# Two-block transformer step on one core: moving the building of the third and fourth block's weight sums to later stages

## The reference, cut to what matters

```python
def second_block(x, c, ...):
    for i in range(2):
        ...
        y = _dsa_mixer(h, ...) if i == 0 else _short_conv_mixer(h, ...)
        x = x + g1 * y
        h = _rmsnorm(x, norm2_g[i]) * (1.0 + sc2) + sh2
        x = x + g2 * ((silu(h @ w_gate[i]) * (h @ w_up[i])) @ w_down[i])
```

## Time and profile before

| | before |
|---|---|
| median of 3 runs | 2673.64 us (2669.71 to 2680.84) |
| the profiled execution's own time | 2684.21 us |
| its span | 2682.4 us |
| PE busy | 2610.3 us (97%) |
| DVE, ACT, POOL busy | 1463.0, 1002.9, 840.7 us |
| mean granted clock of TensorE | 0.986 |
| DMA, software queue | 121.85 MB, 17.4% of the 16 engines' span |
| DMA, hardware queue (SP's loads) | 266.28 MB, 33.2% |

### The profile page before, as it was taken

The page is one execution under the profiler, slowest core; times in us unless marked ns, Lnnn a source line. Parts: engine busy times, 40 slices in busy tenths (PEclk is TensorE's granted clock), DMA queues, the critical chain, the costliest instruction groups (busy, mean ns, idle before and its releaser), DMA issues.

```text
span 2682.4 us, 30812 instructions
## 1 busy us (share of the span) xinstructions
PE 2610.3 (97%) x12482; PEld 2134.7 (80%) x12482; DVE 1463.0 (55%) x2083; ACT 1002.9 (37%) x1606; POOL 840.7 (31%) x702
## 2 busy tenths in 40 slices
PE   9999999999999999999999999969999999999999
PEld 8878887877777778887787666758888888888887
DVE  4343256666666445544577598443336854643366
ACT  4222234334444323422265445522225532322253
POOL 6663025675556678086600241100000000000000
PEclk9999999999999999999999998989999999999999
DMA  6543334455555576364464218899335633333355
GB/s 193 157 142 122 102 115 139 125 159 154 141 134 145 149 204 198 97 177 148 132 210 143 71 48 212 216 265 223 97 94 180 201 92 97 118 103 102 95 167 174
DMA packets 422286, 391.68 MB, mean 146 GB/s; under 512 B 17572, under 2 KB 337312, under 8 KB 422080
## 3 DMA queue, kind: packets, MB, share of 16 engines
q1 hardware_dynamic: 377264, 266.28, 33.2%
q0 software_dynamic: 43344, 121.85, 17.4%
q10 hardware_dynamic: 1536, 1.58, 0.2%
HBM read 385.95 MB, written 71.34 MB: 170 GB/s over the span
## 4 chain that ended last, share of the span: by engine, by line
PE 86%; DVE 7%; DMA 3%; ACT 2%; POOL 2%; issue 1%; DVEq 0%; ACTq 0%; POOLq 0%
PE PS L507 18%; PE PS L508 18%; PE PS L510 16%; PE PS L642 3%; PE PS L645 3%; PE PS L644 3%; PE PS L581 3%; PE PS L582 3%; PE PS L583 3%; PE PS L512 2%; DMA RAW<-in_ffn_w_gate 1%; PE PS L1110 1%; PE PS L544 1%; PE PS L545 1%; PE PS L546 1%; PE PS L1082 1%
## 5 line engine op out<-in xcount | busy, mean ns | idle before, releaser
L507 PE MATMUL PS<-HH,WH 128*128 128x512 f32 x2248 | 898.9, 400 | 0.1
L508 PE MATMUL PS<-HL,WH 128*128 128x512 f32 x2248 | 876.6, 390 | 0.0
L510 PE MATMUL PS<-HH,WL 128*128 128x512 f32 x1967 | 767.9, 390 | 0.0
L1948 DVE TENSOR_TENSOR WL<-RAW,WH 128x1024 fp32r<-128x1024 f32 (+1 forms) x306 | 400.8, 1311 | 516.6 <-ACT WH L1203 516.3
L1203 ACT ACTIVATE WH<-RAW 128x1024 fp32r<-128x1024 f32 (+1 forms) x318 | 330.8, 1042 | 488.0 <-PE PS L512 403.3
L507 PEld LDWEIGHTS PS<-HH,WH 128*128 128x128 f32 x2248 | 423.9, 189 | 106.5 <-issue 21.7
L508 PEld LDWEIGHTS PS<-HL,WH 128*128 128x128 f32 x2248 | 423.8, 189 | 88.5 <-issue 4.6
L510 PEld LDWEIGHTS PS<-HH,WL 128*128 128x128 f32 x1967 | 370.4, 188 | 78.3
L3026 POOL TENSOR_SCALAR ADA<-ADA,CA 128x512 f32<-128x512 f32 x168 | 305.0, 1815 | 30.3 <-DMA ADA<-in_ada_w 25.1
L1948 DVE TENSOR_TENSOR WLr<-RAWD,WHr 128x1024 fp32r<-128x1024 f32 (+1 forms) x142 | 165.2, 1167 | 144.9 <-ACT WHr L1203 144.7
L3023 POOL TENSOR_TENSOR ASUM<-ASUM,ADA 128x512 f32<-128x512 f32 x168 | 235.1, 1399 | 14.1
(11 more groups left out here) (411 smaller groups left out, 3860.9 us busy)
## 6 DMA issues: line engine op xcount, KB each, us to landing
ADA<-in_ada_w POOLq DMA_DIRECT2D x192, 256.0 KB, 3.3
RAW<-in_ffn_w_gate SPq DMA_DIRECT2D x88, 512.0 KB, 3.7
RAW<-in_ffn_w_up SPq DMA_DIRECT2D x88, 512.0 KB, 3.8
RAW<-in_w_in SPq DMA_DIRECT2D x84, 512.0 KB, 4.1
RAWD<-in_ffn_w_down SPq DMA_DIRECT2D x67, 512.0 KB, 3.7
sum<-in_ffn_w_down POOLq DMA_DIRECT2D x12, 2816.0 KB, 21.2
RAWD<-sum SPq DMA_DIRECT2D x60, 512.0 KB, 4.0
sum<-in_ffn_w_down POOLq DMA_DIRECT2D x30, 512.0 KB, 5.9
```

The costliest lines, as they stand in the source:

```text
L507: pe.matmul(PS[:, b, cols], wh[:, k, :], hi[:, k, cols], start=k == 0, stop=False)
L508: pe.matmul(PS[:, b, cols], wh[:, k, :], lo[:, k, cols], start=False, stop=False)
L510: pe.matmul(PS[:, b, cols], wl[:, k, :], hi[:, k, cols], start=False, stop=False)
L1948: return v.tensor_tensor(out, x, y, op).then_inc(*tick("dve", *event))
```

## The change

Before, POOL made the sums of f = 2 and of f = 3 one after the other as soon as its attention work was over. Now it first waits until TensorE has finished the second chunk of F3 and then makes the sums of f = 2; the fourth sums of f = 2 follow; then it waits until TensorE has finished the first chunk of the convolution's projection, makes the sums of f = 3, and goes on to the fourth sums of f = 3.

```diff
@@ -3203,9 +3203,9 @@
     behind.finish()
     for _ in beside:
         pass
-    for f in (2, 3):
-        for _ in make_sums(g, tick, lambda sem: w.wait_ge(*here(sem)), A, f, 1):
-            pass
+    w.wait_ge(*at("mm", F3 + 1))
+    for _ in make_sums(g, tick, lambda sem: w.wait_ge(*here(sem)), A, 2, 1):
+        pass
 
     U8 = m["U8"]
 
@@ -3215,6 +3215,9 @@
             tt(fourth_sum(m, f, i), U8[:, A11, pair(i), :], U8[:, S3, pair(i), :], ALU.subtract, "fourth", f, i)
 
     fourth_sums(2)
+    w.wait_ge(*at("mm", CONV))
+    for _ in make_sums(g, tick, lambda sem: w.wait_ge(*here(sem)), A, 3, 1):
+        pass
     fourth_sums(3)
```

## The result

The changed kernel takes 2701.57 us in the median of 4 runs (2699.72 to 2703.5), the kernel before 2677.06 us in 4 (2669.71 to 2680.84): ratio 1.0095, interval 1.0068 to 1.0122, so 24.5 us slower. A later comparison of the same two kernels gave 2706.32 against 2668.94 us, ratio 1.0123 (1.0078 to 1.0168). The forecast was 2686 with a range up to 2699: the direction and most of the places were right, the size was not.

The account below looks back on a forecast made before the run. TensorE, busy for 97% of the span, was taken as the bound. The terms -25.6 + 17 + 20 gave +11.4, say +12 us: 2696 against the profiled execution, 2686 us in medians, range 2656 to 2699.

Parts of the forecast that it names:

- Together -25.6 us: Boundary before F3: the 22.7 us wait for Y goes, and 2.9 us of half clock with it.
- +17: F3: f = 2's sums delay weight loads; 15 us late plus 2 for half clock, range 11 to 21.
- +20: Convolution: f = 3's sums delay weight loads, chunk 10 being 17 to 20 us late; with the clock, range 14 to 24.
- The attention: 0: Attention: taking f = 2's sums out gains 0, since PE is already busy for 69.96 of 70 us.
- The later, single transfers: 0: F3 and convolution: each set's three last transfers, going one at a time, cost 0.
- The covers: Sums are ready before first read, fourth sums are in time, the boundary before F4 stays free: all 0.
- The loads keep up: F3 and convolution lose under 5 us together, the boundary's gain stays: 2648 to 2653 us; chance 0.12.
- half of it: Only the convolution pays, F3's chunks loaded ahead suffice: about -4, so 2670 us; chance 0.10.
- It goes on: F3 and convolution: later single adds starve TensorE again, up to 4 us each; +29, so 2703 us; chance 0.08.
- The page's price: Sums' transfers: 8.6 us per 2,816 KB, five filling the queue some 35 us, covered by chunks ahead; sum -25.6.

Follow-up runs that it names:

- e_att_conv: Changed kernel, but with f = 2's sums left in the attention as before; 2683.21 us, ratio 1.0042 to the kernel before.
- e_att_f3: Kernel before, but f = 3's sums wait until TensorE has finished F3's second chunk; 2681.95 us, ratio 1.0046 to the kernel before.
- e_hole: Kernel before, but f = 3's sums wait until ACT has made the high parts of F3's first three chunks; 2663.25 us, ratio 0.9938.
- e_none3: Kernel before without f = 3's sums, F4's down products reading f = 2's instead; 2660.69 us, ratio 0.9939 to the kernel before.
- e_serial: Changed kernel, but each transfer of a set waits for the one before it; 2672.01 us, ratio 0.998 to the kernel before.

## Why the prediction was wrong, by its own steps

**"Together -25.6 us", the step that failed.** As a reading of the profiled execution it was exact: the sets' first issue moved by 25.4 us, A1 by 25.8. As a term against the median it was wrong. The prediction took the 10.6 us between that execution and the median as something to be subtracted on both sides. They were part of the term itself: this execution had the longest wait of the four, 22.7 us where the others had 15.3, 5.9 and none. Over the four profiles of before A1 is 193.9, 185.3, 177.0 and 165.5 us, 180.4 in the mean, and 168.1 in the changed kernel, so the boundary gives 12 us in the mean and not 25.6. With -12 the forecast's own sum would have been -12 + 37 = +25, or 2699 from the 2673.6 on which it stood, the edge of its range. Four profiles are few; the two differences of medians, less the 41 us that the two stages cost, leave 17 and 4 us for the boundary. A smaller part of the miss is the base: in the comparison before's median was 2677.06, 3.4 us above that of its first three runs.

**"+17" in F3 and "+20" in the convolution: right in place and kind, 2 us small each.** They cost 19.3 and 21.9 us. Landings 12.4 us apart, ACT waiting for them (for 6.4 to 11.4 us at a time), three waits of PE and then no more came as said, in F3 with three late chunks (9, 10 and 11) where two had been counted. The lateness was well worked out: the last late chunk began 63.3 us after the head's second in F3 (1853.22), 16.9 later than the 46.4 that the prediction wanted, and 63.4 us after the head's first in the convolution (2221.25), 19.7 later than 43.7. It had taken 15 and 18; for F3 its own rows gave 11 to 15, the stated upper end of 18 is not worked out. What it mis-sized is how that time is spent. PE's waits were 12.0 and 15.1 us, where 15 and 18 had been taken. The half clock was not 2 us a stage but 19.3 - 12.0 = 7.3 in F3 and 21.9 - 15.1 = 6.8 in the convolution. The prediction priced one pause; here three pauses of 3 to 6 us follow each other 12.4 us apart, and TensorE works much of the time between them at 1.2 GHz. Windows of the changed kernel, PE alone:

```profile
1820.00:1825.00 5.00, 5.00 (x24) 1.00 1.12 211
1825.00:1830.00 5.00, 2.02 (x8) 0.96 1.12 211
1830.00:1835.00 5.00, 5.00 (x17) 0.70 1.12 212
1835.00:1840.00 5.00, 0.69 (x4) 0.99 1.12 211
1840.00:1845.00 5.00, 4.28 (x10) 0.50 1.12 213
```

From 1830 to 1835 PE is busy throughout and issues 17 matrix multiplies, where 1820 to 1825, at full clock, has 24. Over all three pauses, first in the changed kernel and then 40 undisturbed microseconds of before's F3:

```profile
1825.00:1865.00 40.00, 27.96 (x93) 0.83 1.08 258
...
1900.00:1940.00 40.00, 40.00 (x178) 1.00 0.30 87
```

The 85 matrix multiplies that are missing are, at 5.44 us for 24, the stage's 19.3 us; PE stood for 12.0 of them.

**The attention: 0. Right.** With f = 2's set there, and at most 0.6 us of wait for Y behind it, A1 is 164.1 to 168.3 us (e_att_conv, e_att_f3, e_hole, e_none3), without it 167.8 to 168.5 (the changed kernel, e_serial).

**The later, single transfers: 0. Right.** ACT still waits up to 10.13 us in F3 and 10.47 us in the convolution for a load during them, but no wait of PE comes after the first three of each stage.

**The covers: right.** The first reads of the sums, the fourth sums, and F4's boundary had room in the changed kernel.

**The rivals.** "The loads keep up" and "half of it" fell with the first profile. "It goes on" gave a time near the measured one, 2703, but not by its mechanism: no wait came with the later adds. The clearly slower result had a fourth cause that no rival held: that the kernel before was slower in the profile read than it is in general.

**The page's price.** By the Trainium skill's "DMA: Bandwidth & Descriptors" ("Anatomy of one DMA — SWDGE (gpsimd) path") the change would have been a gain, by an estimate from its fit. The trace and the runs do not agree with it for transfers from DRAM to DRAM: with loads beside it the fifth of f = 2's set in the changed kernel landed 26 us after its issue, where the fit gives 8.6.

Together: 19.3 + 21.9 - 12 = +29 us from the profiles, and the two measured differences of medians are 24.5 and 37.4 us.

## What to carry to other kernels

Where a long wait in a profile hangs on two transfers that are issued within microseconds of each other, take a second profile before its removal is priced: it may be a race that the median mostly wins. Background transfers by DMA need not be moved to a "quiet" stage, since a stage that lives from a steady stream of small-packet loads paid 19 to 23 us for a queue that never ran empty; keep them where TensorE needs few loads (here the attention), start them when the next stage's first chunks have landed and TensorE will need no other for some 40 us (e_hole: one wait, 0.6% faster than before, and runs that spread over 12 us instead of 30), or let each transfer leave a gap before the next. And when work on a queue is paced or stretched, ask again what stands behind it and which boundary it now reaches.

## What the runs showed of the hardware that was not expected

- Half a microsecond in the order of two issues on different queues goes with 7 us of TensorE (copies 0.3 us after the first load: 22.1 us of wait; 0.5 us: 15.3; one profile each).
- DMA engines that are busy all the time (share 1.05 with 254 GB/s) can leave TensorE at 100.00 of 100 us; with a share of 1.12 at 211 GB/s it starved. The adds come in packets of 2 KB (2.66 MB in 1299), the copies in packets of 4 KB (2.88 MB in 720), and while two transfers with adds fill their queue one packet of 512 bytes passes for each of theirs (2793 and 2794).
- Gaps between such transfers repay much: in e_serial the loads moved at 32 GB/s beside an add and at 300 GB/s in the 5 us before it.
- Pauses of 3 to 6 us, 12.4 us apart, cost more than half as much again by the clock as by waiting: 12.0 us of waits went with 19.3 us of lost time in F3, 15.1 with 21.9 in the convolution.
- The kernel before, compared with itself in one job, came out 0.3% apart with an interval that leaves out 1 (1.0009 to 1.0052); by the profiles its runs are no single cluster.
